# FFN up-projection by seven block products for eight in 21 of 22 tiles, with sums of X blocks made by token rows on VectorE

## The chip, the cores and the metric

The kernel runs on one core of one Trainium2 chip. The metric is the device time of one execution in microseconds, and the figure compared is the median of several runs. The core has five engines with a queue of instructions each: TensorE (PE in the profile), VectorE (DVE), ScalarE (ACT), GpSimd (POOL) and SyncE (SP, which here starts the DMAs). Each engine works its queue in order, and the engines wait for each other by semaphores.

## The reference

A trunk of two layers over 1024 tokens of 1024 channels, in float32. Each layer has a token mixer, a LayerNorm, and then the part that is changed:

```python
def conv_ffn(x, w_in, b_in, conv_w, conv_b, w_out, b_out):
    h = x @ w_in + b_in                       # 1024 x 5632
    hp = jnp.pad(h, ((0, 0), (1, 1), (0, 0)))
    h = hp[:, :-2] * conv_w[0] + hp[:, 1:-1] * conv_w[1] + hp[:, 2:] * conv_w[2] + conv_b
    u, g = jnp.split(h, 2, axis=-1)
    return (u * jax.nn.gelu(g, approximate=False)) @ w_out + b_out
...
        x = layer_norm(alpha * x + ff, ln_g[i, 1], ln_b[i, 1])
```

## The kernel before

A product of float32 matrices is made of three products of rounded parts: each operand is split into a high part (rounded to the type fp32r) and a low part (what the rounding left), and high by high, low by high and high by low are summed in PSUM. The input X of the FFN lies turned in SBUF as `XTh` and `XTl`: 128 channels of one of KT = 8 groups across the partitions, 1024 tokens along them.

`ffn_stage` runs once in each layer. The 2816 hidden channels of `u` and of `g` are FT = 22 tiles of 128. A tile f has a column block of `w_in` for u and one for g. `up_tile` (L1118) makes one of these two: for each half of the tokens, 8 channel groups times 3 products, so 48 matmuls of 128x512 into `ph`, and 96 for both. Then, for each tile:

- ScalarE (`take`, L1224) copies `ph` to `H` with the bias added, and to `C` with the middle tap of the convolution applied.
- VectorE (`conv`, L1284) adds the left tap (L1289) and the right tap (L1294), each one instruction of 128x1024 on `H` and `C` in SBUF.
- ScalarE applies GELU to the g half (`gate`, L1239), VectorE multiplies the halves (L1307), ScalarE rounds the product into `Ah` (`high`, L1243), VectorE makes the low part `Al` (`low`, L1311).
- After every second tile `down` (L1134) multiplies the two finished tiles by their rows of `w_out`: 16 outputs of 128x512, each 6 matmuls, in four PSUM banks `po` in turn. VectorE adds each output to the residual X (`add`, L1282). The output r waits until output r - 4 has been added. The last four tiles are summed in one go (`down_four`, L1157).

GpSimd prepares all weights: `split` (L1064) rounds 128x1024 weights of a DMA buffer `raw_weights` (two slots) into a high part (L1069, one input) and subtracts for the low part (L1071, two inputs). Three such splits belong to each tile. The order of everything is written out by hand. In the steady state a loop (`Fori`) holds a round of two up tiles, one `down` and their surroundings; its body is `round_` on TensorE (L1196). At the start of the stage GpSimd also adds the output bias to X (`add_bias`), between the splits, and ScalarE scales X by alpha (L1221).

## Time and profile before

| | us |
|---|---|
| median of 3 runs (2929.1 to 2930.05) | 2929.44 |
| the profiled execution, its own time | 2936.39 |
| its span in the trace | 2934.6 |
| PE busy (share of the span) | 2766.2 (94%) |
| DVE busy | 1644.1 (56%) |
| ACT busy | 993.6 (34%) |
| POOL busy | 1244.3 (42%) |
| mean granted TensorE clock | 0.972 |
| FFN of layer 0, first matmul to last part of the turned result | 799.5 to 1547.5 |
| FFN of layer 1, first matmul on | 2193.3 to the end |

A busy time is a sum of durations. A 128x512 matmul has a modelled duration of 390 ns, but one follows the other every 227 ns, so the cadence, not the duration, tells what a matmul costs. Idle time of an engine is put down to the engine or DMA that released it.

### The profile page before, as it was taken

The page shows a single profiled execution, that of the slowest core. Times are in us where ns is not written, and L with a number is a line of the kernel's source. Part 1 is how long each engine was busy: PE and PEld are TensorE (multiplying, and loading weights), DVE is VectorE, ACT ScalarE, POOL GpSimd, SP SyncE. Part 2 cuts the span into 40 slices and gives each one's busy share as a digit, 9 for nine tenths or more (in the row PEclk, how much of TensorE's full clock was granted, in tenths as well). Part 3 has the DMA queues.
Part 4 walks back from the last instruction along what each step waited for, and adds up shares of the span by engine and source line. Part 5 has one row for each costly group of instructions (what it writes and reads, how often), then busy time and mean ns, then how long its engine had stood idle before and what let it go on. Part 6 is the DMA issues. An engine that isn't in the chain of part 4 may idle for free. (4 is left out here: it accounts for less than half of the span.)

```text
span 2934.6 us, 36448 instructions
## 1 busy us (share of the span) xinstructions
PE 2766.2 (94%) x13387; PEld 2303.8 (79%) x13387; DVE 1644.1 (56%) x2106; ACT 993.6 (34%) x1402; POOL 1244.3 (42%) x890
## 2 busy tenths in 40 slices
PE   7999999977899999999998999998789999999998
PEld 6788888866788888888877888887668888888886
DVE  3676666663664444444473777777466444444446
ACT  3545554542231111221223555555323111222222
POOL 2444444323472333333354566654356233332335
PEclk9999999978999999999999999998899999999999
DMA  3100001225021111111121221211602111111111
GB/s 112 31 22 29 29 29 30 55 63 199 22 66 44 43 57 50 43 50 50 43 86 43 55 60 42 50 44 22 213 22 66 43 43 55 52 43 50 50 43 72
DMA packets 212649, 163.16 MB, mean 56 GB/s; under 512 B 34939, under 2 KB 194251, under 8 KB 212555
## 3 DMA queue, kind: packets, MB, share of 16 engines
q1 hardware_dynamic: 212411, 161.38, 18.6%
q8 instruction: 59, 0.97, 0.1%
q10 hardware_dynamic: 144, 0.52, 0.0%
q14 instruction: 35, 0.29, 0.0%
HBM read 137.24 MB, written 24.64 MB: 55 GB/s over the span
## 5 line engine op out<-in xcount | busy, mean ns | idle before, releaser
L1131 PE MATMUL ff_ph<-XTh,WH 128*128 128x512 f32 x1408 | 550.1, 391 | 6.8 <-PEq L41 6.8
L1131 PE MATMUL ff_ph<-XTl,WH 128*128 128x512 f32 x1408 | 549.3, 390 | 0.0
L1131 PE MATMUL ff_ph<-XTh,WL 128*128 128x512 f32 x1408 | 549.2, 390 | 0.0
L1289 DVE SCALAR_TENSOR_TENSOR ff_C<-ff_H,ff_par,ff_C 128x1024 f32<-128x1024 f32 x88 | 206.2, 2344 | 548.3 <-ACT ff_C L1233 548.3
L1069 POOL TENSOR_SCALAR WH<-raw_weights 128x1024 fp32r<-128x1024 f32 x128 | 142.2, 1111 | 847.1 <-PE ff_ph L1131 490.1
L1071 POOL TENSOR_TENSOR WL<-raw_weights,WH 128x1024 fp32r<-128x1024 f32 x128 | 328.7, 2568 | 10.7
L1131 PEld LDWEIGHTS ff_ph<-XTh,WH 128*128 128x128 f32 x1408 | 265.3, 188 | 62.7 <-issue 7.6
L1131 PEld LDWEIGHTS ff_ph<-XTh,WL 128*128 128x128 f32 x1408 | 265.2, 188 | 55.5
L1131 PEld LDWEIGHTS ff_ph<-XTl,WH 128*128 128x128 f32 x1408 | 265.4, 189 | 55.1
L1229 ACT ACTIVATE ff_H<-ff_ph,ff_par 128x1024 f32<-128x1024 f32 x88 | 98.4, 1118 | 553.7 <-PE ff_ph L1131 553.7
L1282 DVE TENSOR_TENSOR X<-ff_po,X 128x512 f32<-128x512 f32 x288 | 191.6, 684 | 102.5 <-PE ff_po L1145 102.5
L1145 PE MATMUL ff_po<-WH 128*128 128x512 f32 x576 | 228.2, 396 | 4.6
L1145 PE MATMUL ff_po<-WH,WL 128*128 128x512 f32 x576 | 224.5, 390 | 0.0
L1145 PE MATMUL ff_po<-WL,WH 128*128 128x512 f32 x576 | 224.3, 389 | 0.0
L547 ACT ACTIVATE da_E<-da_S,da_mn 128x1024 f32<-128x1024 f32 x128 | 142.9, 1117 | 227.8 <-DVE da_mn L660 225.0
L1526 POOL TENSOR_SCALAR na_E<-na_E,na_rden 128x512 f32<-128x512 f32 x128 | 104.7, 818 | 194.1 <-DVE na_rden L1869 193.4
L278 POOL TENSOR_SCALAR da_E<-da_E,da_rden,da_neglam 128x1024 f32<-128x1024 f32 x64 | 76.6, 1196 | 202.1 <-DVE da_rden L674 202.1
L347 PE MATMUL da_pa<-XTh,da_wh 128*128 128x512 f32 x360 | 152.2, 423 | 10.0 <-POOL da_wl L272 3.8
L660 DVE CUSTOM_DVE_ANT_0 da_S<-da_S,da_strip 128x1024 f32<-128x1024 f32 x128 | 153.8, 1241 | 8.1 <-PE da_S L361 8.0
L1612 PE MATMUL na_pa<-XTh,na_wh 128*128 128x512 f32 x360 | 145.6, 404 | 8.3 <-DVE na_wl L1847 6.9
L1243 ACT ACTIVATE WH<-ff_C 128x1024 fp32r<-128x1024 f32 x44 | 46.8, 1063 | 306.5 <-PE ff_po L1145 269.0
L347 PE MATMUL da_pa<-XTh,da_wl 128*128 128x512 f32 x360 | 144.1, 400 | 0.0
(224 smaller groups left out, 5993.4 us busy)
## 6 DMA issues: line engine op xcount, KB each, us to landing
raw_weights<-in_ffn_w_in SPq DMA_DIRECT2D x88, 512.0 KB, 3.8
raw_weights<-in_ffn_w_out SPq DMA_DIRECT2D x44, 512.0 KB, 3.6
raw_weights<-in_attn_w_qkv SPq DMA_DIRECT2D x24, 512.0 KB
raw_weights<-in_na_w_qkv SPq DMA_DIRECT2D x24, 512.0 KB, 4.4
wo_oraw<-heads_t SPq DMA_DIRECT2D x16, 512.0 KB, 4.4
rpb_rows<-da_rows SPq DMA_DIRECT2D x2, 3840.0 KB, 26.7
na_B<-rpb_rows SPq DMA_DIRECT2D x32, 224.0 KB, 4.3
da_E<-in_x SPq DMA_DIRECT2D x8, 512.0 KB, 5.7
```

The source lines that it names most:

```text
L347: last = nc.tensor.matmul(out[:], w[:, j // 2, k], x[:, k, t0:t0 + BANK], start=(i == 0), stop=(i == 3 * KT - 1))
L547: nc.scalar.activation(E[:, t % 2, c], Sc[c][:], ACT.Exp, scale=-1.0, bias=mn[:, t % 2, c:c + 1], accum_out=den[:, t % 2, c:c + 1]).then_i ...
L660: nc.vector.tensor_tensor_reduce(out=Sc[c][:], in0=Sc[c][:], in1=strip[:, (QT - 1 - t) * P:(QT - 1 - t) * P + S], scale=1.0, scalar=3.0e38 ...
L1069: nc.gpsimd.tensor_scalar(wh[:, slot], wraw[:, raw_slot], 1.0, 1.0, ALU.mult, ALU.mult).then_inc(w_high, 1)
L1071: nc.gpsimd.tensor_tensor(out=wl[:, slot], in0=wraw[:, raw_slot], in1=wh[:, slot].bitcast(F32), op=ALU.subtract).then_inc(w_low, 1)
L1131: last = nc.tensor.matmul(out[:, at], wt[:, slot, k * P:(k + 1) * P], x[:, k, at], start=(k == 0 and n == 0), stop=(k == KT - 1 and n == 2))
L1145: last = nc.tensor.matmul(po[r % 4][:], a[:, f, t * P:(t + 1) * P], wt[:, slots[f], half * BANK:(half + 1) * BANK], start=(f == 0 and n == ...
L1229: nc.scalar.activation(H[:, parity, 1:S + 1], ph[parity][:].rearrange("p k n -> p (k n)"), ACT.Identity, bias=par[:, 0, bass.ds(idx, 1)])
L1282: nc.vector.tensor_tensor(out=at, in0=po[r % 4][:], in1=at, op=ALU.add).then_inc(added, 1)
L1289: nc.vector.scalar_tensor_tensor(out=c, in0=h[:, 0:S], scalar=tap[1], in1=c, op0=ALU.mult, op1=ALU.add).then_inc(conv_link, 1)
L1526: nc.gpsimd.tensor_scalar(E[:, b], E[:, b], rden[:, b:b + 1], 1.0, ALU.mult, ALU.mult).then_inc(scaled, 1)
L1612: last = nc.tensor.matmul(out[:], w[:, j // 2, k], x[:, k, t0:t0 + BANK], start=(i == 0), stop=(i == 3 * KT - 1))
```

## The change

Tile 0 is made as before, with 96 matmuls, in four pieces (`up_plain`). For tiles 1 to 21 the product of a 256-column block (128 of u, 128 of g) by X is seen as a 2 by 2 by 2 block product (two gates, two halves of the channels, two halves of the tokens), and made by Strassen's scheme with seven products M1 to M7 of half-size blocks. `up_seven` has for each tile seven calls of `multiply`, each 4 channel groups times 3 products, 12 matmuls: 84 for 96.

What comes with it:

- Sums of weights (quads): five of the seven products need a sum or difference of two weight blocks, which GpSimd makes for every tile (`quad_add`). The rounding to the high part moves to ScalarE (`quad_copy`), the low part stays on GpSimd (`quad_lower`). They live in four slots (`SLOTS`). A quad takes its slot when the product four places earlier is made. All of these are 128x512. The rows of `w_out` are rounded on ScalarE (`down_copy`) and lowered on GpSimd (`down_lower`, 128x1024).
- Sums of X blocks, once in a stage: B1, B3, B4 and B7 are summed by token rows on VectorE (`mix_tokens`, 128x2048), turned by TensorE into PSUM (`turn_mix`, 16 transposes of 128x128 each), rounded by ScalarE (`mix_copy`) and lowered by VectorE (`mix_lower`). B6 is summed by TensorE (`sum_mix`, 16 matmuls of 128x512 with an identity).
- The results are put together from the products: ScalarE keeps M5 and M2 in SBUF (`keep`), VectorE forms U (`sum_u`, two instructions) and then `cross_take`, `main_prepare` and `main_take`, two of each, all 128x512 with one operand in PSUM. ScalarE reads the middle tap from `H` in SBUF (`centre_tap`) where it read PSUM.
- The loops are written out as straight code, and the LayerNorm's gain rows are loaded late in the stage.

```diff
+        token_mixes = {B1: (tokens(1, 1), tokens(2, 2), ALU.add, in_c), B3: (tokens(1, 2), tokens(2, 2), ALU.subtract, in_h),
+                       B4: (tokens(2, 1), tokens(1, 1), ALU.subtract, in_c), B7: (tokens(2, 1), tokens(2, 2), ALU.add, in_d)}
+        moving = {M5: quarter[2, 2], M2: quarter[1, 1], M1: places[B1], M3: places[B3], M4: places[B4],
+                  M7: quarter[2, 1], M6: quarter[1, 2]}
...
+            def quad_add(f, j):
+
+                n, i = f - PLAIN, index(f, j)
+                a, b, op = {M5: ((0, 1), (0, 2), ALU.add), M2: ((1, 1), (1, 2), ALU.add), M1: ((0, 1), (1, 2), ALU.add),
+                            M7: ((0, 2), (1, 2), ALU.subtract), M6: ((1, 1), (0, 1), ALU.subtract)}[j]
+                for gate, k in (a, b):
+                    pool.wait_ge(piece_in[2 * gate + k - 1], 16 * (n + 1))
+                if i >= SLOTS:
+                    pool.wait_ge(made, i - SLOTS + 1)
+                nc.gpsimd.tensor_tensor(out=Rf[:, i % SLOTS], in0=quad(*a), in1=quad(*b), op=op).then_inc(quad_sum, 1)
+
+            def quad_lower(f, j):
+
+                i = index(f, j)
+                pool.wait_ge(quad_high, i + 1)
+                src = quad(0, 1) if j == M3 else quad(1, 2) if j == M4 else Rf[:, i % SLOTS]
+                nc.gpsimd.tensor_tensor(out=Rl[:, i % SLOTS], in0=src, in1=Rh[:, i % SLOTS].bitcast(F32),
+                                        op=ALU.subtract).then_inc(quad_low, 1)
...
+            def next_quads(f):
+                quad_add(f, M5)
+                quad_add(f, M2)
+                quad_lower(f, M5)
+                quad_add(f, M1)
+                quad_lower(f, M2)
+                quad_lower(f, M1)
+                quad_lower(f, M3)
+
+            next_quads(PLAIN)
+            for t in range(TT):
+                add_bias(t)
+            for f in range(PLAIN, FT):
+                quad_lower(f, M4)
+                quad_add(f, M7)
+                quad_add(f, M6)
+                quad_lower(f, M7)
+                quad_lower(f, M6)
+                down_lower(f - 1)
+                if f + 1 < FT:
+                    next_quads(f + 1)
+            down_lower(FT - 1)
...
+            def multiply(f, j, out):
+
+                i = index(f, j)
+                pe.wait_ge(quad_low, i + 1)
+                xh, xl = moving[j]
+                for k in range(HK):
+                    wh, wl = (part[:, i % SLOTS, k * P:(k + 1) * P] for part in (Rh, Rl))
+                    for n, (w, x) in enumerate(((wh, xh), (wh, xl), (wl, xh))):
+                        last = nc.tensor.matmul(out, w, x[:, k], start=(k == 0 and n == 0),
+                                                stop=(k == HK - 1 and n == 2))
+                last.then_inc(made, 1)
...
+            def up_seven(f):
+
+                n = f - PLAIN
+                if n:
+                    pe.wait_ge(cross_h, 2 * n - 1)
+                else:
+                    pe.wait_ge(up_out, 2 * PLAIN)
+                multiply(f, M5, P12)
+                if n:
+                    pe.wait_ge(cross_h, 2 * n)
+                multiply(f, M2, P21)
+                if n:
+                    pe.wait_ge(main_h, 2 * n - 1)
+                else:
+                    sum_mix(B6)
+                    pe.wait_ge(mix_low, 2 * B1 + 2)
+                multiply(f, M1, P11)
+                pe.wait_ge(kept, 2 * n + 1)
+                if n == 0:
+                    pe.wait_ge(mix_low, 2 * B3 + 2)
+                multiply(f, M3, P12)
+                pe.wait_ge(kept, 2 * n + 2)
+                if n == 0:
+                    pe.wait_ge(mix_low, 2 * B4 + 2)
+                multiply(f, M4, P21)
+                pe.wait_ge(u_first, n + 1)
+                if n == 0:
+                    pe.wait_ge(mix_low, 2 * B7 + 2)
+                multiply(f, M7, P11)
+                if n:
+                    pe.wait_ge(main_h, 2 * n)
+                else:
+                    pe.wait_ge(mix_low, 2 * B6 + 2)
+                multiply(f, M6, P22)
...
+            up_plain(0, 0)
+            turn_mix(B1)
+            up_plain(0, 1)
+            turn_mix(B3)
+            up_plain(1, 0)
+            turn_mix(B4)
+            up_plain(1, 1)
+            turn_mix(B7)
+            for f in range(PLAIN, FT):
+                up_seven(f)
+                if f % 2 == 0 and f < FT - 2:
+                    down(f // 2 - 1)
+            down_four()
 
...
+            def centre_tap(f, parity):
+                n, idx = f - PLAIN, f + parity * FT
+                act.wait_ge(a_low, f)
+                act.wait_ge(cross_h, 2 * n + 1 + parity)
+                act.wait_ge(main_h, 2 * n + 1 + parity)
+                nc.scalar.activation(C[:, parity], H[:, parity, 1:S + 1], ACT.Identity, bias=par[:, 4, idx:idx + 1],
+                                     scale=par[:, 2, idx:idx + 1]).then_inc(tapped, 1)
...
+            for f in range(PLAIN, FT):
+                behind_down = f % 2 == 1 and 3 <= f < FT - 1
+                if behind_down:
+                    high(f - 1)
+                keep(f, M5)
+                quad_copy(f, M4)
+                keep(f, M2)
+                if f == PLAIN:
+                    mix_copy(B6)
+                quad_copy(f, M7)
+                quad_copy(f, M6)
+                if not behind_down:
+                    gate(f - 1)
+                if f < FT - 1:
+                    down_copy(f - 1)
+                if not behind_down:
+                    high(f - 1)
+                if f + 1 < FT:
+                    quad_copy(f + 1, M5)
+                    quad_copy(f + 1, M2)
+                    quad_copy(f + 1, M1)
+                else:
+                    down_copy(FT - 2)
+                    down_copy(FT - 1)
+                centre_tap(f, 0)
+                if f + 1 < FT:
+                    quad_copy(f + 1, M3)
+                centre_tap(f, 1)
+                if f % 2 == 0 and f < FT - 2:
+                    gate(f)
...
+                nc.vector.tensor_tensor(out=U, in0=P11, in1=part[:, 0], op=ALU.subtract).then_inc(u_first, 1)
...
+            def cross_take(f, parity):
+                idx = f + parity * FT
+                dve.wait_ge(made, index(f, M4 if parity else M3) + 1)
+                dve.wait_ge(conv_done, 2 * f - 1 + parity)
+                nc.vector.scalar_tensor_tensor(out=H[:, parity, here(1 - parity)], in0=(P12, P21)[parity],
+                                               scalar=par[:, 0, idx:idx + 1], in1=part[:, parity], op0=ALU.add,
+                                               op1=ALU.add).then_inc(cross_h, 1)
...
+            def main_take(f, parity):
+                n = f - PLAIN
+                dve.wait_ge(made, index(f, M6 if parity else M7) + 1)
+                dve.wait_ge(main_part, 2 * n + 2 - parity)
+                nc.vector.scalar_tensor_tensor(out=H[:, parity, here(parity)], in0=(P11, P22)[parity],
+                                               scalar=delta[:, parity, f:f + 1], in1=H[:, parity, here(parity)], op0=ALU.add,
+                                               op1=ALU.add).then_inc(main_h, 1)
```

On GpSimd, in the round of an even tile f. Before, three splits to a tile, each a rounding and a subtraction (two of them here, from the start of layer 1's stage, with the bias adds between); ff_bias is the output bias:

```order
L1069 TENSOR_SCALAR WH<-raw_weights 128x1024
L1071 TENSOR_TENSOR WL<-raw_weights,WH 128x1024
L1079 TENSOR_TENSOR X<-X,ff_bias 128x1024 x2
L1069 TENSOR_SCALAR WH<-raw_weights 128x1024
L1071 TENSOR_TENSOR WL<-raw_weights,WH 128x1024
```

Now, for one tile and the first quads of the next (ff_Rlf is the sum of weights, ff_Rh and ff_Rl its high and low part, ff_WDlf a row block of `w_out`):

```order
L1172 TENSOR_TENSOR ff_Rlf<-raw_weights 128x512 x2
L1179 TENSOR_TENSOR ff_Rl<-ff_Rlf,ff_Rh 128x512 x2
L1186 TENSOR_TENSOR ff_WDl<-ff_WDlf,ff_WDh 128x1024
L1172 TENSOR_TENSOR ff_Rlf<-raw_weights 128x512 x2
L1179 TENSOR_TENSOR ff_Rl<-ff_Rlf,ff_Rh 128x512
L1172 TENSOR_TENSOR ff_Rlf<-raw_weights 128x512
L1179 TENSOR_TENSOR ff_Rl<-ff_Rlf,ff_Rh 128x512 x2
L1179 TENSOR_TENSOR ff_Rl<-raw_weights,ff_Rh 128x512 x2
```

The roundings have left the engine, and twelve instructions of half the width with two inputs, and one of full width, stand for each tile.

On VectorE, around the same `down`. Before, the taps of an up tile stood close behind it and most of the adds to X behind them (ff_C is the convolved tile, ff_po the output of `down`):

```order
L1282 TENSOR_TENSOR X<-ff_po,X 128x512
L1294 ISA
L1294 SCALAR_TENSOR_TENSOR ff_C<-ff_H,ff_par,ff_C 128x1024
L1281 REGISTER_ALU
L1282 TENSOR_TENSOR X<-ff_po,X 128x512
L1281 REGISTER_ALU
L1282 TENSOR_TENSOR X<-ff_po,X 128x512
```

Now, from the last part of tile f - 1 on (ff_ph holds the seven products, ff_H the tile before its taps):

```order
L1542 TENSOR_TENSOR ff_C<-ff_C 128x1024
L1572 SCALAR_TENSOR_TENSOR ff_H<-ff_ph,ff_par,ff_part 128x512
L1580 TENSOR_TENSOR ff_H<-ff_po,ff_H 128x512
L1547 TENSOR_TENSOR WL<-ff_C,WH 128x1024
L1587 SCALAR_TENSOR_TENSOR ff_H<-ff_ph,ff_delta,ff_H 128x512 x2
L1531 SCALAR_TENSOR_TENSOR ff_C<-ff_H,ff_par,ff_C 128x1024
L1523 TENSOR_TENSOR X<-ff_po,X 128x512 x2
L1537 SCALAR_TENSOR_TENSOR ff_C<-ff_H,ff_par,ff_C 128x1024
L1523 TENSOR_TENSOR X<-ff_po,X 128x512 x2
```

The first add of a `down` (L1523) stands behind the left tap (L1531) of the tile that TensorE has only just finished, and that tap needs ScalarE's `centre_tap`.

On ScalarE, where `centre_tap` (L1443) stands in the even tile:

```order
L1426 ACTIVATE ff_Rh<-ff_Rlf 128x512 x2
L1392 ACTIVATE ff_C<-ff_C 128x1024
L1413 ACTIVATE ff_WDh<-ff_WDlf 128x1024
L1400 ACTIVATE WH<-ff_C 128x1024
L1426 ACTIVATE ff_Rh<-ff_Rlf 128x512 x3
L1443 ACTIVATE ff_C<-ff_H,ff_par 128x1024
L1426 ACTIVATE ff_Rh<-raw_weights 128x512
L1443 ACTIVATE ff_C<-ff_H,ff_par 128x1024
```

Three roundings of the next tile's sums (L1426) stand ahead of it, so it comes after GpSimd's third sum for the next tile.

## Rows read from the trace of the kernel before

**Rows 1.** Busy time in a stretch of the first FFN stage, each engine (instructions).
```profile
core 0: us, PE busy (x) PEld busy (x) DVE busy (x) ACT busy (x) POOL busy (x), PEclk, DMA share, GB/s
1000.00:1200.00 200.00, 199.20 (x872) 162.98 (x872) 88.96 (x84) 40.90 (x38) 66.35 (x38) 1.00 0.15 47
```

**Rows 2.** Chain of work that ended last: start, us, engine, tile, line, instructions.
```profile
2732.47 15.26 PE ff_po L1145 x66
2747.73 43.53 PE ff_ph L1131 x192
```

**Rows 3.** Waits in the first FFN stage: who for whom, us, times, longest.
```profile
PEld ff_po L1145 <- DVE X L1282: 10.0, 18, 0.6
```

**Rows 4.** Groups by form, VectorE, whole span.
```profile
L1289 DVE SCALAR_TENSOR_TENSOR ff_C<-ff_H,ff_par,ff_C 128x1024 f32<-128x1024 f32 x88 | 206.2, 2344 | 548.3 <-ACT ff_C L1233 548.3
L1282 DVE TENSOR_TENSOR X<-ff_po,X 128x512 f32<-128x512 f32 x288 | 191.6, 684 | 102.5 <-PE ff_po L1145 102.5
```

**Rows 5.** Single lines: durations ns min/median/max.
```profile
L1289 DVE SCALAR_TENSOR_TENSOR ff_C<-ff_H,ff_par,ff_C x88: 1285/2380/3407, 822.9 to 2881.4; 128x1024 f32<-128x1024 f32 x88
...
L1071 POOL TENSOR_TENSOR WL<-raw_weights,WH x128: 2387/2397/3337, 806.1 to 2880.5; 128x1024 fp32r<-128x1024 f32 x128
...
L1510 POOL TENSOR_TENSOR na_B<-na_colmask,na_B x16: 2112/2473/3092, 1559.7 to 2040.8; 128x896 f32<-128x896 f32 x16
```

**Rows 6.** In order of time, VectorE and GpSimd, 847 to 853 us.
```profile
847.86 1.47 DVE L1289 SCALAR_TENSOR_TENSOR ff_C<-ff_H,ff_par,ff_C 128x1024 f32<-128x1024 f32 x1 [0.51 <-ACT ff_C L1233]
848.34 3.24 POOL L1071 TENSOR_TENSOR WL<-raw_weights,WH 128x1024 fp32r<-128x1024 f32 x1
849.37 3.29 DVE L1294 SCALAR_TENSOR_TENSOR ff_C<-ff_H,ff_par,ff_C 128x1024 f32<-128x1024 f32 x1
```

**Rows 7.** Groups by form, ScalarE, whole span.
```profile
L1233 ACT ACTIVATE ff_C<-ff_ph,ff_centre,ff_par 128x1024 f32<-128x1024 f32 x88 | 105.6, 1200 | 7.7 <-DVE WL L1311 7.7
...
L1740 ACT ACTIVATE na_PT<-na_tb 128x512 fp32r<-128x512 f32 x128 | 76.4, 597 | 77.3 <-PE na_tb L1648 76.0
...
L1239 ACT ACTIVATE ff_C<-ff_C 128x1024 f32<-128x1024 f32 x44 | 46.7, 1060 | 190.2 <-DVE ff_C L1294 190.2
```

**Rows 8.** In order of time, TensorE, after waits of 2.6 and 3.8 us.
```profile
35.29 0.79 PE L347 MATMUL da_pa<-XTh,da_wh 128*128 128x512 f32 x1 [2.63 <-DVE XTl L583]
35.88 0.63 PE L347 MATMUL da_pa<-XTl,da_wh 128*128 128x512 f32 x1
36.31 0.63 PE L347 MATMUL da_pa<-XTh,da_wl 128*128 128x512 f32 x1
...
38.38 0.39 PE L347 MATMUL da_pa<-XTl,da_wh 128*128 128x512 f32 x1
38.61 0.39 PE L347 MATMUL da_pa<-XTh,da_wl 128*128 128x512 f32 x1
...
62.48 0.77 PE L347 MATMUL da_pa<-XTh,da_wh 128*128 128x512 f32 x1 [3.76 <-POOL da_wl L272]
...
65.60 0.39 PE L347 MATMUL da_pa<-XTl,da_wh 128*128 128x512 f32 x1
```

**Rows 9.** In order of time, TensorE, after two waits of 1.6 us.
```profile
158.14 1.09 PE L376 MATMUL da_tb<-ident,da_raw 128*128 128x128 f32 x8 [1.57 <-DVE da_ATl L608]
...
159.31 0.39 PE L347 MATMUL da_pa<-XTl,da_wh 128*128 128x512 f32 x1
...
310.03 1.09 PE L376 MATMUL da_tb<-ident,da_raw 128*128 128x128 f32 x8 [1.56 <-DVE da_ATl L608]
...
311.46 0.63 PE L347 MATMUL da_pa<-XTh,da_wl 128*128 128x512 f32 x1
```

**Rows 10.** In order of time, TensorE: transposes between matmuls.
```profile
23.52 1.91 PE L443 MATMUL da_S<-ident,da_E 128*128 128x128 f32 x16
```

**Rows 11.** DMA issues of the page: KB each, median us to landing.
```profile
raw_weights<-in_ffn_w_in SPq DMA_DIRECT2D x88, 512.0 KB, 3.8
```

More of the change, by code:

```diff
@@ new lines, in products @@
+            def products(out, r, f0, n, first, last_f):
+                t, half = r // 2, r % 2
+                for f in range(f0, f0 + n):
+                    (ah, al), (wh, wl, _) = a_slot(f), d_slot(f)
+                    for j, (a, w) in enumerate(((ah, wh), (ah, wl), (al, wh))):
+                        last = nc.tensor.matmul(out, a[:, t * P:(t + 1) * P], w[:, half * BANK:(half + 1) * BANK],
+                                                start=(f == first and j == 0), stop=(f == last_f and j == 2))
+                return last
@@ L1138, in down @@
+            def down(i):
+                pe.wait_ge(down_low, 2 * i + 2)
                 pe.wait_ge(a_low, 2 * i + 2)
                 for r in range(OUTS):
[L1140 to L1141 removed]
+                    if i or r >= 4:
                         pe.wait_ge(added, OUTS * i + r - 3)
[L1143 to L1147 removed]
@@ L1331, in add_last @@
+            f = FT - 1
+            left(f, 0), right(f, 0), left(f, 1), right(f, 1)
+            product(f)
+            low(f)
             def add_last(r):
```

584 lines of the change are left out of this document (353 added, 231 removed).

## The prediction

> **What bounds the kernel now.** I read the busy time by stretch first. In 200 us of an FFN stage TensorE is busy for 199.2 and starts 872 matmuls at a granted clock of 1.00, so one matmul costs 200 / 872 = 0.229 us there; VectorE is busy 44%, GpSimd 33%, ScalarE 20% [rows 1]. The chain of waits that ended last says the same: two tiles are 192 matmuls in 43.53 us, 0.227 each, and then a `down` [rows 2]. Over a round of 288 matmuls the two figures differ by 0.7 us. TensorE alone sets the time. Its only regular wait in the stage is for the adds of `down`, twice in each of the 9 `down`s of the stage [rows 3], and that is the 0.7. Matmuls taken away here are time won, as long as nothing else becomes late.
>
> So the second question is what else is near. The groups of VectorE have one odd figure: the left tap takes 2344 ns on average [rows 4], though the shortest of its kind took 1285 [rows 5]. The rows in order of time show why. At 848.34 GpSimd starts a subtraction, two inputs in SBUF; at 849.37 VectorE starts a right tap, also two inputs in SBUF. The tap ends at 852.66, 1.1 us after GpSimd's instruction (851.58), and GpSimd's own ran 3.24 where 2.39 is its shortest, since the tap before it ended only at 849.33 [rows 6]. Instructions of the two engines that both read two tensors in SBUF run one at a time, in order of arrival, each holding the other for about 1.07 us (a 1024 wide one of VectorE) or 2.25 us (GpSimd). VectorE's adds from PSUM are untouched: 684 ns on average [rows 4]. Nothing of this is on TensorE's path today.
>
> **The change part by part.** Sums are for one layer, then doubled.
>
> Matmuls removed: 21 tiles x 12 = 252, by 0.227 = -57.2 us. Added: `sum_mix` 16 x 0.227 = 3.6; four `turn_mix` of 16 transposes, 1.91 each [rows 10] = 7.6. Net on TensorE: -46.0 us.
>
> GpSimd: a tile has 12 instructions of 512 and one of 1024, all with two inputs. A 512 wide one is not in the trace. From 2112 ns at 896 and 2387 at 1024 [rows 5], 2.15 ns an element and 0.19 fixed, it is 1.29 us; the bounds are half of 2.39 (1.20) and 1.40, a fixed part of 0.4. A tile costs GpSimd 12 x 1.29 + 2.39 = 17.9 us, and TensorE needs 84 x 0.227 = 19.1 us for it. VectorE's six two-input instructions of a tile (four taps, product, low part) hold GpSimd off 6 x 1.07 = 6.4 us more: 24.3 us for a tile of 19.1 us. Over two tiles with a `down` (59.9 us) it fits, as does VectorE: 12 two-input ones of 1.3, 16 adds and 16 new 512 wide ones that read PSUM like the adds, 0.7 each, 38 us. In the even tile alone, which carries the odd tile's taps and comes before `down`, it does not.
>
> I walk that tile, T being the start of its M5. ScalarE's centre tap and quad copy after the previous M6, then GpSimd's lowering of M3 with one hold by a tap, bring GpSimd to the lowering of M4 at about T + 5.2. From there it has no free moment: nine instructions of 512 until the third sum for the next tile (lower M4, add M7, add M6, lower M7, lower M6, add M5, add M2, lower M5, add M1) = 11.6, the `w_out` one 2.4, and five holds by the right, left and right taps, product and low part, 1.07 less 0.12 that overlaps, = 4.7. The third sum ends at T + 23.9. ScalarE stands behind it: the copy 0.6 (512 wide, [rows 7]), then `centre_tap`, 1.06 plus 0.1 each for its bias and scale, 1.25 [rows 7]. VectorE's left tap follows, 1.3 and a 0.4 hold, then the first add 0.7. With 0.1 for handing over, less where instructions overlap, the add is done at T + 28. TensorE meets its wait for that add at output 4 of `down`: 19.1 + 24 x 0.227 = T + 24.5. Wait: 3.5 by 1.29, 3.2 by the mean with 1.25; I take 3.2.
>
> What such a wait costs beyond itself: after 2.63 us of waiting TensorE's matmuls followed each other every 0.43 us, from 35.29 to 38.38, and after 3.76 us from 62.48 to 65.60, where 0.23 is the rule [rows 8]: granted 1.2 GHz for 3.1 us, so 7 matmuls in the time of 14, 1.6 us lost. After 1.57 us the fall is the exception: 158.14 runs on at full level, 310.03 falls [rows 9]. At 3.2 I expect the fall each time. With 0.1 for the restart, a `down` costs 3.2 + 0.1 + 1.6 = 4.9, in 9 downs 44.1; the wait of today, 9 x 0.7, goes: +37.8 us.
>
> Two tile pairs have no `down` between them and both are heavy, 1 to 2 and 20 to 21. There M5 needs its low part, which GpSimd ends at about T + 22.4, where TensorE asks at T + 19.1: 3.0 + 1.6 each, the first partly in one slow stretch with others: +9 us.
>
> The start: after tile 0's last piece TensorE turns B7 (1.9) and waits for ScalarE, which has scaled four rows of X (four of 1.05) and then takes the second half (1.12 + 1.20 [rows 7]): about 2.8, a clock fall of 1.6 and 0.9 at an earlier turn: +5.3. The bias adds (8 on GpSimd) end before M4 of tile 1 needs its low part; they are covered by tile 0's 96 matmuls and cost nothing, and about 1 us a piece if that cover is short. The end: tile 21's taps, product, rounding and low part all come after its last product, against 48 matmuls (11 us) of cover: +1.
>
> DMAs: the quads are issued in halves of 256 KB. Today's 512 KB take 3.8 us to land [rows 11] and a slot is free at least 8 us ahead. The holds on SP's queue (a `w_out` load stands ahead of the next tile's pieces and waits for a `down` just finished) are covered; if they were not, each us would show as a wait at M5. The straight code for the loops: nothing, since the straight-line attention stage holds the same 0.23 cadence [rows 8].
>
> Sum: -46.0 + 37.8 + 9 + 5.3 + 1 = +7.1 us a layer, **+14.2** in all. The profiled execution took 2936.39 (1.8 beside its span), so 2950.6; it lies 7 above the median of the runs, 2929.44, and against that the same difference gives **2944**. This result is the difference of two large numbers, so its bounds matter: 0.05 us on the 512 wide instruction moves the wait by 0.5 us, and 18 waits by 9 us.
>
> A page of the Trainium skill bears on that instruction. The rows say 1.29 us, by a line through 896 and 1024 elements [rows 5]. GPSIMD Engine Reference, section "Elementwise — side-by-side cycle accounting", states 4497 ns for a two-input add of 2048 float32 against 2293 on VectorE, and advises VectorE for elementwise work. A line from that figure through the trace's 2387 at 1024 would make 512 wide 1.33 us, an estimate by that page, the waits 0.4 longer and the sum about +21. It speaks against the change, and the trace decides.
>
> **The rivals.**
>
> A. *The clock holds through the waits.* The waits are there, but TensorE comes back at 2.4 GHz as at 158.14 [rows 9]. Then 12 falls of 1.6 are missing in each layer: 7.1 - 19.2 = -12.1, twice -24: 2905. Against it: both waits of 2.6 us and more were followed by one [rows 8].
>
> B. *The waits are short.* If a 512 wide instruction takes 1.20 and handing over costs less, the chain is 1.5 us shorter: waits of about 1.7, clock mostly kept. -46.0 + 9 x 1.8 - 6.3 + 2 x 1.5 + 4 = -29 a layer: 2871, and up to 2905 if some fall. For it: nothing but the unmeasured 512. Against: 2112 at 896.
>
> C. *GpSimd and VectorE hold each other less at half width*, since a hold lasts half as long. Then only the start waits: -46.0 + 4 - 6.3 = -48 a layer: 2833. Against: a hold is per instruction, and GpSimd queues one behind the other.
>
> D. *GpSimd becomes the bound.* With 1.40 or more for a 512 wide one, or loads landing late, every tile pair waits at M5 too, and the `down` wait is 4.3: 9 x 1.1 + 9 x 0.8 = 17 more a layer: 2978. It decides from about 1.35 us.
>
> That the seven products are not what runs is excluded by the order of TensorE's queue.
>
> **How the numbers follow.** Forecast (2920 to 2962) 0.54; A 0.16; B 0.14; C 0.06; D 0.10. The predicted time is the forecast's, 2944. Its own range, 0.3 us on the wait either way (11) and 0.3 on what a fall costs (11), is 2920 to 2962 with both the same way. The range 2880 to 2975 leaves out C, half of D and part of B. A measurement tells 0.2%, 5.9 us, from no change. Slower: most of the forecast (0.47) and D, 0.57; same 0.07 from the forecast and 0.03 from A, 0.10; faster the rest, 0.33.
>
> **What would show it.** In the profile after: `multiply` matmuls 84 a tile at 0.227; GpSimd's 512 wide subtractions at 1.29 shortest and about 2.2 where held; a wait of TensorE for VectorE's add once in each `down`, about 3 us, 18 times, with `centre_tap` late behind the quad copies; the granted clock in the FFN stretches at 0.95 to 0.97 instead of 1.00. Wrong would be: no such wait, or a clock of 1.00 behind it (A), or waits at `multiply` in every tile (D).

## The result

The changed kernel took 2947.47 us (median of 4 runs, 2945.85 to 2950.84), the kernel before 2929.74 on the same chip (4 runs, 2929.10 to 2931.75). The ratio is 1.0061, 95% interval 1.0043 to 1.0078: slower by 0.6%. The profiled execution took 2948.5, its span 2946.7 at a mean granted clock of 0.962, where before had 0.972.

From a stage's first matmul to its last, the FFN stages took 745.4 and 729.4 us before (layer 0 and layer 1) and take 754.6 and 735.4 now: 9.2 and 6.0 us longer. The rest of the program took 3.1 us less in this execution than in that of before.

One stretch of the FFN stage, the same 200 us as [rows 1], and the stretch behind it, with the same columns:

```profile
1000.00:1200.00 200.00, 190.07 (x808) 155.16 (x807) 127.71 (x135) 65.72 (x86) 128.41 (x80) 0.97 0.17 50
1200.00:1400.00 200.00, 190.04 (x813) 155.15 (x812) 127.79 (x136) 64.71 (x85) 129.45 (x81) 0.97 0.16 48
```

TensorE stands idle for 9.9 us of 200 where it stood idle for 0.8, and its matmuls are slower too. 813 matmuls at the 0.2284 of [rows 1] (199.20 / 872) would be 185.7, and they took 190.04: 4.3 us lost in three rounds here, 5.5 (190.07 - 184.6) in the stretch before. VectorE went from 44% to 64%, GpSimd from 33% to 64%. What TensorE waits for in the FFN stages, whole span (who for whom, us in total, times, longest), answers to [rows 3]:

```profile
PE ff_po L1310 <- DVE X L1523: 57.9, 18, 3.3
...
PE ff_ph L1265 <- POOL ff_Rl L1179: 12.1, 4, 3.5
...
PE ff_ph L1265 <- ACT ff_C L1387: 5.2, 2, 2.6
...
PE ff_po L1310 <- DVE WL L1547: 3.7, 2, 2.2
```

The first line is the one of the 18 `down`s, at output 4, for VectorE's add. The second is M5 of tiles 2 and 21 of each layer, the third the start of tile 1, the fourth the end of the stage. Durations of GpSimd's lines (min/median/max in ns), for [rows 5]:

```profile
L1172 POOL TENSOR_TENSOR ff_Rlf<-raw_weights x210: 1261/1289/2299, 803.2 to 2879.4; 128x512 f32<-128x512 f32 x105
...
L1179 POOL TENSOR_TENSOR ff_Rl<-raw_weights,ff_Rh x84: 1280/2266/3344, 810.7 to 2874.9; 128x512 fp32r<-128x512 f32 x84
```

The chain behind one such wait, in order of time (start, us, engine, line). M5 of this even tile began at 1117.8, which is T of the prediction. The lower half of M4 is the second of the two instructions at 1120.88; the first took 2.29 us, so it starts at about 1123.1, T + 5.3. GpSimd, from there to its third sum:

```profile
1120.88 4.51 POOL L1179 TENSOR_TENSOR ff_Rl<-raw_weights,ff_Rh 128x512 fp32r<-128x512 f32 x2
1125.36 3.52 POOL L1172 TENSOR_TENSOR ff_Rlf<-raw_weights 128x512 f32<-128x512 f32 x2
1128.84 3.53 POOL L1179 TENSOR_TENSOR ff_Rl<-ff_Rlf,ff_Rh 128x512 fp32r<-128x512 f32 x2
1132.34 3.39 POOL L1186 TENSOR_TENSOR ff_WDl<-ff_WDlf,ff_WDh 128x1024 fp32r<-128x1024 f32 x1
1135.70 3.53 POOL L1172 TENSOR_TENSOR ff_Rlf<-raw_weights 128x512 f32<-128x512 f32 x2
1139.18 1.29 POOL L1179 TENSOR_TENSOR ff_Rl<-ff_Rlf,ff_Rh 128x512 fp32r<-128x512 f32 x1
1140.43 1.29 POOL L1172 TENSOR_TENSOR ff_Rlf<-raw_weights 128x512 f32<-128x512 f32 x1
```

No row has an idle time in brackets: GpSimd never stood still. Then ScalarE, VectorE and TensorE:

```profile
1141.76 0.63 ACT L1426 ACTIVATE ff_Rh<-ff_Rlf 128x512 fp32r<-128x512 f32 x1 [1.87 <-POOL ff_Rlf L1172]
1142.29 1.23 ACT L1443 ACTIVATE ff_C<-ff_H,ff_par 128x1024 f32<-128x1024 f32 x1
```
```profile
1143.55 1.73 DVE L1531 SCALAR_TENSOR_TENSOR ff_C<-ff_H,ff_par,ff_C 128x1024 f32<-128x1024 f32 x1 [5.42 <-ACT ff_C L1443]
1145.21 1.27 DVE L1523 TENSOR_TENSOR X<-ff_po,X 128x512 f32<-128x512 f32 x2
```
```profile
1145.94 0.50 PE L1310 MATMUL ff_po<-ff_WDh,WH 128*128 128x512 f32 x1 [3.32 <-DVE X L1523]
...
1147.72 0.63 PE L1310 MATMUL ff_po<-ff_WDh,WH 128*128 128x512 f32 x1
1148.14 0.63 PE L1310 MATMUL ff_po<-ff_WDl,WH 128*128 128x512 f32 x1
1148.57 0.63 PE L1310 MATMUL ff_po<-ff_WDh,WL 128*128 128x512 f32 x1
```

The copy of the third sum, the centre tap directly behind it, the left tap, the add, and TensorE after 3.32 us; then matmuls every 0.43 us, TensorE's lower level of 1.2 GHz, where 0.23 is the rule. VectorE stood idle for 5.42 us before the left tap: it is not the slow one, it is handed its input late.

### The profile page after: what moved, and what is told of

It is laid out like the page before. It is cut to its first block and busy times, and to the rows that moved or that the text cites. A ratio compares the mean times of both kernels' runs of the same rounds, so it can differ in the third digit from the quotient of the medians.

```text
span 2946.7 us, 35802 instructions
## 1 busy us (share of the span) xinstructions
PE 2703.4 (92%) x13043; PEld 2251.2 (76%) x13043; DVE 1919.8 (65%) x2474; ACT 1187.3 (40%) x1762; POOL 1654.8 (56%) x1182
## 5 line engine op out<-in xcount | busy, mean ns | idle before, releaser
L1179 POOL TENSOR_TENSOR ff_Rl<-raw_weights,ff_Rh 128x512 fp32r<-128x512 f32 x84 | 172.3, 2060 | 388.7 <-ACT ff_Rh L1426 388.7
L1172 POOL TENSOR_TENSOR ff_Rlf<-raw_weights 128x512 f32<-128x512 f32 x210 | 311.3, 1495 | 51.4 <-PE ff_ph L1265 36.9
L1310 PE MATMUL ff_po<-ff_WDh,WH 128*128 128x512 f32 x624 | 258.3, 414 | 57.9 <-DVE X L1523 57.9
L1426 ACT ACTIVATE ff_Rh<-ff_Rlf 128x512 fp32r<-128x512 f32 x210 | 132.8, 633 | 419.6 <-POOL ff_Rlf L1172 419.6
L1179 POOL TENSOR_TENSOR ff_Rl<-ff_Rlf,ff_Rh 128x512 fp32r<-128x512 f32 x210 | 291.3, 1404 | 0.0
L1265 PE MATMUL ff_ph<-XTh,ff_Rh 128*128 128x512 f32 x672 | 266.0, 396 | 17.4 <-POOL ff_Rl L1179 12.1
L1265 PE MATMUL ff_ph<-XTl,ff_Rh 128*128 128x512 f32 x672 | 264.5, 394 | 0.0
L1265 PE MATMUL ff_ph<-XTh,ff_Rl 128*128 128x512 f32 x672 | 264.0, 393 | 0.0
L1310 PE MATMUL ff_po<-ff_WDl,WH 128*128 128x512 f32 x624 | 253.4, 406 | 0.0
L1310 PE MATMUL ff_po<-ff_WDh,WL 128*128 128x512 f32 x624 | 252.9, 405 | 0.0
L1531 DVE SCALAR_TENSOR_TENSOR ff_C<-ff_H,ff_par,ff_C 128x1024 f32<-128x1024 f32 x88 | 155.9, 1772 | 144.5 <-ACT ff_C L1443 143.1
L1523 DVE TENSOR_TENSOR X<-ff_po,X 128x512 f32<-128x512 f32 x288 | 192.9, 685 | 80.5 <-PE ff_po L1310 80.1
L1265 PE MATMUL ff_ph<-WH,ff_Rl 128*128 128x512 f32 x504 | 196.1, 389 | 0.0
L1265 PE MATMUL ff_ph<-WL,ff_Rh 128*128 128x512 f32 x504 | 196.1, 389 | 0.0
```

The lines of the kernel that those rows point to most:

```text
L1172: nc.gpsimd.tensor_tensor(out=Rf[:, i % SLOTS], in0=quad(*a), in1=quad(*b), op=op).then_inc(quad_sum, 1)
L1179: nc.gpsimd.tensor_tensor(out=Rl[:, i % SLOTS], in0=src, in1=Rh[:, i % SLOTS].bitcast(F32), op=ALU.subtract).then_inc(quad_low, 1)
L1265: last = nc.tensor.matmul(out, w, x[:, k], start=(k == 0 and n == 0), stop=(k == HK - 1 and n == 2))
L1310: last = nc.tensor.matmul(out, a[:, t * P:(t + 1) * P], w[:, half * BANK:(half + 1) * BANK], start=(f == first and j == 0), stop=(f == las ...
L1426: nc.scalar.activation(Rh[:, i % SLOTS], src, ACT.Copy).then_inc(quad_high, 1)
L1523: nc.vector.tensor_tensor(out=at, in0=po[:, r % 4], in1=at, op=ALU.add).then_inc(added, 1)
```

## The experiments

The question is what makes the 18 waits, what each costs beyond itself, and where the gain of the smaller product count went. Theory 1 is the prediction's chain: GpSimd without a gap, held off by VectorE's two-input instructions; ScalarE's copies in order behind GpSimd's sums; the centre tap behind the copies; the left tap; the add; and a fall of the clock. The rivals are the place of the adds on VectorE, GpSimd's own throughput, and a clock that has nothing to do with these waits. Every kernel is a small edit of the changed kernel. The changed kernel itself was measured only on the first chip, at 1.0061 of the kernel before. So on a chip where before takes 2934.24 us the changed kernel is taken at 2952, and where before takes 2931.22 at 2949. By the interval of that ratio these two figures are good to about 5 us, and so are all differences from the changed kernel below. The slow intervals that are counted below are steps of about 0.43 us, in place of 0.23, from one matmul of a `down` to the next; each loses 0.2 us. In the changed kernel a fall of the clock follows 16 of the 18 waits, with 117 slow intervals in all.

### 1. The centre tap ahead of the quad copies (ScalarE)

```
+                early = f % 2 == 0 and f < FT - 2
+                if early:
+                    centre_tap(f, 0)
                 if f + 1 < FT:
                     quad_copy(f + 1, M5)
                     quad_copy(f + 1, M2)
                     quad_copy(f + 1, M1)
...
-                centre_tap(f, 0)
+                if not early:
+                    centre_tap(f, 0)
```

> One thing is changed against the changed kernel: in even tiles that have a `down`, ScalarE issues centre_tap(f, 0) before the three quad_copy of the next tile (M5, M2, M1) and not behind them. Theory 1 (the chain GpSimd's third sum, ScalarE's copy of it, centre tap, left tap, add sets the wait): the 18 waits of 3.3 us for VectorE's add at output 4 go, and the clock's fall behind each (5 to 13 intervals at 0.43 in place of 0.22 us, about 1.6 us) goes with them: 18 x 4.9 = 88 us less than the changed kernel's 2947.5, about 2859 us, unless the three copies, now later, make a new wait at M5 of the next tile. Rival (the place of the adds behind the left tap on VectorE is the cause, whatever ScalarE does): the wait stays above 2 us and the time above 2930 us. Rival (GpSimd as the bound, 105 us of work per pair of tiles): the time moves to M5 or M2 of the odd tiles, and the gain is under 20 us.

Measured: 2863.03 us (2862.39 to 2863.78) against 2934.24 of before, ratio 0.9760 (0.9745 to 0.9775). Against the changed kernel that is 89 us less, where 88 were expected. The line for VectorE's add is gone from TensorE's waits; those for GpSimd (12.1, 4 times) are as they were, so no new one took its place. In the middle of the layer TensorE is never idle:

```profile
1000.00:1200.00 200.00, 200.00 (x878) 164.02 (x877) 146.40 (x152) 68.00 (x90) 139.77 (x84) 1.00 0.16 48
1200.00:1400.00 200.00, 200.00 (x879) 164.32 (x879) 135.99 (x142) 70.08 (x93) 143.56 (x88) 1.00 0.19 58
```

The same place of an even tile, ScalarE and GpSimd in order of time:

```profile
1179.15 1.25 ACT L1443 ACTIVATE ff_C<-ff_H,ff_par 128x1024 f32<-128x1024 f32 x1 [3.03 <-DVE ff_H L1591]
1180.30 1.15 ACT L1426 ACTIVATE ff_Rh<-ff_Rlf 128x512 fp32r<-128x512 f32 x2
1184.30 0.63 ACT L1426 ACTIVATE ff_Rh<-ff_Rlf 128x512 fp32r<-128x512 f32 x1 [2.85 <-POOL ff_Rlf L1172]
```
```profile
1182.99 1.28 POOL L1172 TENSOR_TENSOR ff_Rlf<-raw_weights 128x512 f32<-128x512 f32 x1
```

The third sum starts at 1182.99, 3.8 us after the tap and 23.6 us after M5 of its tile, where it was 22.6 in the changed kernel. It is as late as ever, even 1.0 us later: the lower half before it waits 0.2 us for its copy and takes 2.0 us for 1.3, beside the left tap. It no longer matters: its product is due only after a whole `down` and two more products. The copies that moved behind the tap had room; the tap had none. GpSimd was not the bound; the order on ScalarE made its lateness count.

### 2. The adds ahead of the left tap (VectorE)

```
-                    left(f, 0)
                     ... add(done), add(done + 1)
+                    left(f, 0)
```

> One thing is changed against the changed kernel: VectorE issues the adds of outputs 0 and 1 of each `down` before the left tap of that tile and not behind it; centre_tap stays late. Theory 1: the left tap is still late by what centre_tap is late, and the adds of outputs 2 and 3 stand behind it, so the wait goes from output 4 to output 6, about 3 us long, less the left tap's own 0.7: 18 x 0.7 = 12 us less, about 2935 us. Rival (the adds' place is the cause): all 18 waits and their falls go, 2859 us.

Measured: 2944.41 us, ratio 1.0030 (1.0019 to 1.0040), 8 us less than the changed kernel where 12 were expected. TensorE's wait is still there 18 times, shorter by 0.5 us in the mean:

```profile
PE ff_po L1310 <- DVE X L1523: 49.2, 18, 2.9
```

The two adds that were freed only bring TensorE to the next two, which still stand behind the left tap: the wait is now at output 6. A fall follows all 18 waits, with 134 slow intervals for 117, so that about 3 us of the 8.7 that the waits lost went back to the clock. The place of the adds on VectorE is worth about 8 us of 89; the lateness of the tap is the rest.

### 3. Matmuls in the time of the wait

```
                 for r in range(OUTS):
                     ...
+                    if r == 4:
+                        for _ in range(14):
+                            nc.tensor.matmul(P12, plus[:], XTh[:, 0, 0:BANK], start=True, stop=True)
                     (wait for the add)
```

> Added to the changed kernel: 14 matmuls of 512 columns into a bank whose contents are not needed any more, in each `down` ahead of the wait at output 4 (about 14 x 0.22 = 3.1 us of the 3.3 us that TensorE stands idle). Nothing else moves, and the wait for the add ends when it did. If the clock falls because TensorE stands idle there, the 5 to 13 intervals at 0.43 us behind 17 of the 18 waits become 0.22 us: 17 x 1.5 = 26 us less, about 2921 us, and the span's mean granted clock goes from 0.96 to about 0.98. Rival (the falls are not from these waits, or the clock holds through such waits and the slow matmuls have another cause): about 2947 us or up to 5 us more, clock unchanged.

Measured: 2925.0 us (2922.05 to 2927.02), ratio 0.9969 (0.9958 to 0.9980), 27 us less with 252 matmuls more; 26 were expected. A stretch in the middle of the layer:

```profile
1200.00:1400.00 200.00, 199.49 (x873) 163.05 (x872) 129.16 (x138) 67.70 (x89) 132.03 (x83) 1.00 0.16 48
```

Granted clock 1.00 for 0.97, and 873 matmuls for 813, of which 14 a `down` are the added ones. No `down` has a slow interval. So of the 89 us of the waits, 27 are the clock's falls (the 117 slow intervals alone make 23) and about 62 the waits themselves (57.9, and what it takes to come back from them). Work that is thrown away made the kernel faster; the early tap shows that it is better not to wait.

### 4. Two of VectorE's instructions in the odd tile made short

This kernel leaves out nearly all of the right taps of the odd tiles, so its convolution isn't complete.

```
+                n = 16 if f % 2 == 1 and f < FT - 1 else S
-                ... scalar_tensor_tensor(out=C[:, parity], in0=H[:, parity, 2:S + 2], ...
+                ... scalar_tensor_tensor(out=C[:, parity, 0:n], in0=H[:, parity, 2:n + 2], ...
```

> Left out against the changed kernel: the right taps of the odd tiles' convolution, all but 16 of 1024 columns (two VectorE instructions for each pair of tiles), so part of the convolution isn't computed. This tells whether GpSimd's additions are late because VectorE's two-operand instructions hold them. Theory 1 (each such VectorE instruction of 1024 columns holds GpSimd's running instruction by about 1.0 us, and those of the odd tile push GpSimd's queue of the even tile back): the wait at output 4 shrinks from 3.3 to about 1.6 us, and half or more of the falls behind it go: 18 x 1.7 + 18 x 0.8 to 1.6 = 45 to 60 us less, 2885 to 2900 us. Rival (GpSimd's own work is the delay and VectorE's doesn't touch it): GpSimd's additions keep their mean durations, the wait stays at 3.3 us, and the time stays within 5 us of 2947.

Measured: 2886.54 us (2885.64 to 2887.86), ratio 0.9839 (0.9824 to 0.9854), 65 us less; 45 to 60 were expected. Nothing was taken from TensorE, from ScalarE or from GpSimd; only 40 VectorE instructions that ran beside them were cut to 16 of their 1024 columns, and the line of the wait is halved:

```profile
PE ff_po L1310 <- DVE X L1523: 28.0, 18, 1.6
```

GpSimd's subtractions from the raw quads, which run beside these taps, fell from a mean of 2060 to 1853 ns, those from the sums from 1404 to 1314. VectorE's work delays GpSimd's, and it comes out at TensorE. These waits account for 29.9 us, those for GpSimd at M5 (8.3 us for 12.1) for 3.8. The granted clock is 1.00 from 1000 to 1400 us, where the changed kernel has 0.97, and none of the 18 `down`s has a fall: behind waits of 1.6 us all of them went (27 by experiment 3), not half, which is the part that I had too low.

### 5. The tap one place later

```
                     quad_copy(f + 1, M5)
                     quad_copy(f + 1, M2)
+                    if f % 2 == 0 and f < FT - 2:
+                        centre_tap(f, 0)
                     quad_copy(f + 1, M1)
...
-                centre_tap(f, 0)
+                if f % 2 or f == FT - 2:
+                    centre_tap(f, 0)
```

> As the kernel of the early centre tap, but centre_tap(f, 0) stands one place later on ScalarE: behind quad_copy M5 and M2 of the next tile, ahead of M1 alone. Theory 1 (each copy holds the tap up until GpSimd's sum for it is there; the third sum alone accounts for over half of the 3.3 us): a `down` waits about 1.0 us at output 4 and 0.7 us at output 6, with few falls of the clock: 18 x 1.7 = 31 us more than the early tap, about 2894 us and about 55 us less than the changed kernel on the same chip. Rival (any place behind GpSimd's sums costs the same, since the sums stand ready together): the whole wait of 3.3 us is back and the time is near 2950 us. Rival (the third sum is the whole cause): no wait, 2863 us.

Measured: 2891.09 us (2889.18 to 2892.02), ratio 0.9860 (0.9844 to 0.9875), 58 us less than the changed kernel and 28 to 29 more than the early tap (ratios 0.9860 and 0.9760). The wait is now at two outputs and short:

```profile
PE ff_po L1310 <- DVE X L1526: 21.6, 34, 0.9
```

None of the 18 `down`s has a fall behind these waits, and the waits are shorter than the 1.7 us a `down` that were expected (21.6 / 18 = 1.2). With the tap behind no copy, two, or all three the kernel stands at 0.976, 0.986 and 1.006. The third sum alone is two thirds of the loss, which fits a chain with GpSimd's instructions as its links, and neither rival of this run.

### 6. and 7. One more addition on GpSimd, without and with the early tap

```
+                if j == M6 and f % 2 == 0:
+                    nc.gpsimd.tensor_tensor(out=Rf[:, i % SLOTS], in0=quad(*a), in1=quad(*b), op=op).then_inc(extra_done, 1)
+                    pool.wait_ge(extra_done, f // 2)
```

> Added to the changed kernel: one more GpSimd addition of two 128x512 operands (1.29 us alone) in each even tile, ahead of the sum for M6. Theory 1 (GpSimd's queue runs without a gap from the lower half of M4 to the third sum of the next tile, and a delay goes on to TensorE in full): 19 x 1.3 = 25 us more, 1.0 us of each as a new wait at M7 of the even tile and 0.4 us as a longer wait at output 4 (3.7 us): ratio to the kernel before about 1.015, near 2975 us. Rival (GpSimd has slack, being busy 56% of the span): no more than 3 us more, ratio 1.006.

> The kernel of the early centre tap with the same additional GpSimd addition in each even tile. If moving the tap took GpSimd off the critical path altogether, the time stays within 3 us of 2863. Theory 1: behind the tap there is no chain any more, but the lower half of M7 in the even tile still comes just in time, so that each pair of tiles waits 1.0 us there and a little behind it: 18 x 1.3 = 23 us more, about 2886 us, with a wait for GpSimd at M7 and none at output 4.

Measured with the early tap: 2885.22 us (2883.49 to 2886.43), ratio 0.9840 (0.9825 to 0.9855), 0.0080 or 23 us above the early tap alone. 23 were expected, and the new wait for GpSimd at a product is there, 18 times about 0.9 us on top of the four of before:

```profile
PE ff_ph L1269 <- POOL ff_Rl L1183: 28.8, 22, 3.6
```

So GpSimd does have a second place where it is just in time, M7 of the even tile, although it is busy for only 59% of the span.

Measured without the early tap: 2950.09 us (2945.45 to 2957.88), ratio 1.0058 (1.0042 to 1.0073), no more than the changed kernel's 1.0061. This missed: 1.015 was expected, and the number is the rival's 1.006. The rival's reason, that GpSimd has slack, is not what the trace shows, since the waits at M7 came as expected; those at output 4 did not grow by the expected 0.4 us (59.1 / 18 = 3.28 for 3.22):

```profile
PE ff_po L1314 <- DVE X L1527: 59.1, 18, 3.3
PE ff_ph L1269 <- POOL ff_Rl L1183: 28.9, 22, 3.6
```

These are 88.0 us for the 70.0 of the changed kernel. What gave most of that back is the clock: 7 of the 18 `down`s have a fall for 16, and 52 slow intervals for 117, about 13 us. In a stretch where both kernels wait 3.3 us in each `down`, the kernel with the addition, and behind it the changed one:

```profile
1120.00:1320.00 200.00, 187.42 (x818) 152.58 (x817) 124.67 (x134) 66.38 (x88) 133.58 (x87) 1.00 0.16 48
```
```profile
1120.00:1320.00 200.00, 190.04 (x813) 155.19 (x812) 128.42 (x135) 67.56 (x90) 129.43 (x81) 0.97 0.16 48
```

And one wait, with the matmuls behind it at 0.23 us from the first on:

```profile
1282.52 0.50 PE L1314 MATMUL ff_po<-ff_WDh,WH 128*128 128x512 f32 x1 [3.28 <-DVE X L1527]
1282.86 0.40 PE L1314 MATMUL ff_po<-ff_WDl,WH 128*128 128x512 f32 x1
1283.09 0.39 PE L1314 MATMUL ff_po<-ff_WDh,WL 128*128 128x512 f32 x1
1283.32 0.40 PE L1314 MATMUL ff_po<-ff_WDh,WH 128*128 128x512 f32 x1
```

The same wait for the same engine, and no fall. The falls that are left are in the first three `down`s of layer 0 and the first four of layer 1. The profiled execution was the longest of this kernel's four, 2957.88 us, and its span is 9.4 us longer than the changed kernel's, so how much of the 18 us came back is known only to some us. Two more kernels ask why the falls went.

### 8. and 9. Is it the length of the tile pair or the pause at M7 that keeps the clock up?

The first adds six matmuls behind the last output of each `down`, meant to make the pair of tiles as long as in experiment 6, with no pause at M7. The second is the kernel of experiment 6 with four matmuls in the pause at M7.

```
                     products(po[:, r % 4], r, 2 * i, 2, 2 * i, 2 * i + 1).then_inc(down_done, 1)
+                for _ in range(6):
+                    nc.tensor.matmul(P12, plus[:], XTh[:, 0, 0:BANK], start=True, stop=True)
```
```
+                if n and f % 2 == 0:
+                    for _ in range(4):
+                        nc.tensor.matmul(P11, plus[:], XTh[:, 0, 0:BANK], start=True, stop=True)
                 multiply(f, M7, P11)
```

> Added to the changed kernel: 6 matmuls of 512 columns into a bank that is not needed any more, behind the last output of each `down`, where TensorE doesn't wait: 18 x 6 x 0.227 = 24.5 us more work. In the kernel with the additional GpSimd addition TensorE stood 1.0 us longer in each pair of tiles, the waits at output 4 were still 3.3 us, and most falls of the clock behind them were gone, so that it took no longer. Theory A (a wait of 3.3 us brings a fall, whatever stands elsewhere in the pair of tiles): falls as in the changed kernel, granted clock 0.97 in the middle of the layer, ratio to the kernel before about 1.006 + 0.008 = 1.0145. Theory B (whether a fall comes hangs on where the waits stand in time, not on their length alone; the pair of tiles is now as long as in that kernel): waits of 3.3 us without falls, granted clock 1.00 in the middle of the layer, 24.5 - 18 x 1.4 = about 0 us more, ratio 1.005 to 1.008.

> The kernel with the additional GpSimd addition, and 4 matmuls of 512 columns (0.9 us) ahead of M7 in each even tile, into M7's own bank, in the time in which TensorE waited 1.0 us there. The pair of tiles keeps its length and the wait of 3.3 us at output 4; only the earlier pause is filled. If the distance of the waits in time decides whether the clock falls, nothing changes: granted clock 1.00 in the second half of the layer, ratio to the kernel before 1.006. If the earlier pause of 1.0 us was what kept the falls away, they are back, granted clock 0.97, and the time is 10 to 20 us longer: ratio 1.009 to 1.013.

Measured, six matmuls behind the outputs: 2973.47 us (2971.02 to 2975.78), ratio 1.0129 (1.0113 to 1.0146), 20 us above the changed kernel for 24.5 us of work. The 18 waits are as in the changed kernel (58.1 us in all), and so are the falls: 15 of 18 `down`s have one, with 113 slow intervals for 117. The interval of the ratio holds theory A's 1.0145 and not theory B's 1.005 to 1.008. A stretch in the middle of the layer:

```profile
1120.00:1320.00 200.00, 190.05 (x821) 155.36 (x820) 125.22 (x134) 64.11 (x84) 127.08 (x80) 0.98 0.16 50
```

Measured, the pause filled: 2954.96 us (2951.68 to 2957.72), ratio 1.0083 (1.0066 to 1.0099), its profiled span 2954.6 beside 2956.1 without the filling. The ratio lies between the two that were expected (1.006, and 1.009 to 1.013) and doesn't decide; the trace does. The falls did not come back, 5 of the 18 `down`s have one for 7 without the filling:

```profile
1120.00:1320.00 200.00, 190.17 (x829) 154.63 (x828) 125.52 (x135) 65.02 (x86) 133.52 (x86) 1.00 0.16 48
```

So the pause at M7 is not what keeps the clock up, and a wait's length alone is not either: four kernels have 18 waits of up to 3.3 us at the same place, and falls behind 16 (the changed kernel), 7 (experiment 6), 15 (experiment 8) and 5 (experiment 9) of them. Where the waits stand in time is left as a candidate, and it is not shown. From one wait to the next it is 64.8 us in the part of experiment 6 without falls and 64.9 in that of experiment 9, 65.2 with the falls in the changed kernel and 66.4 in experiment 8; but in experiment 8 a fall stood at 1353.72, 65.0 us after a wait without one, and in experiment 2 the waits follow each other every 64.8 us with a fall behind each. No one distance parts the two cases. The six matmuls were meant to set the distance alone and did not bring it about, so I can't say which distance does; this stays open.

### 10. The early tap and an earlier start

```
-                    pe.wait_ge(up_out, 2 * PLAIN)
+                    pe.wait_ge(up_out, 2 * PLAIN - 1)
                 multiply(f, M5, P12)
                 if n:
                     pe.wait_ge(cross_h, 2 * n)
+                else:
+                    pe.wait_ge(up_out, 2 * PLAIN)
```

> The kernel of the early centre tap, and at the head of each layer M5 of tile 1 waits for the first of ScalarE's two takes of tile 0 alone (its bank is the first that is free), and M2 for the second. The wait of 2.6 us for ScalarE at M5 goes; M1 then waits for its lower half about 1 us longer than it did at M5 of tile 2: about 2.3 us less a layer, 4 to 5 us less than the early tap alone, 2858 us. Rival (the wait only moves on to the next wait for GpSimd in tile 1 or 2): 2863 us.

Measured: 2859.09 us (2856.43 to 2859.98), ratio 0.9751 (0.9737 to 0.9764). The wait for ScalarE is gone, and GpSimd's went from 12.1 us in 4 to 14.4 in 5. The profiled spans differ by 3.9 us (2857.4 and 2861.3), as expected, but the intervals overlap, so that this step is not told from nothing with certainty. It is the fastest kernel of the study: 2.5% faster than the kernel before.

## Why the prediction was right

Forecast 2944, measured 2947.47; profiled execution forecast 2950.6, measured 2948.5. By its own steps:

- *The price of a 512 wide GpSimd instruction*, 1.29 us by the line through 896 and 1024, was the term on which everything hung. Measured: a median of 1289 ns for the sums and 1293 for the subtractions from them. The estimate of 1.33 by the figure in the Trainium skill's GPSIMD Engine Reference, section "Elementwise — side-by-side cycle accounting", was 3% too long. The totals don't tell its +21 from the +14 of the rows by themselves: the profiled executions differ by 12 (2948.5 less 2936.39), the FFN stages by 15.2, the medians by 17.7.
- *The walk through the even tile.* Lower half of M4 forecast at T + 5.2, third sum ended at T + 23.9, add done at T + 28, TensorE at output 4 at T + 24.5. With T = 1117.8: 5.3, 23.9 (1140.43 + 1.29), 28.1 (1145.94) and 24.8 (1145.94 - 3.32). The order of the chain is the one that was written down.
- *The wait*, 3.2: 57.9 / 18 = 3.22. It is 3.3 in eight of the first layer's nine and 2.5 in the first.
- *The fall behind it*, 1.6 each time: 1.4 to 1.8 for each round in the two stretches, 27 us in all by filling the wait, so 1.5 for each of 18. But the first `down` of a layer had none, one of the others had one twice as long (13 slow intervals), and experiment 6 shows that "each time" was luck of the arrangement. Both waits of [rows 8] had a fall and one of the two of [rows 9] had, and the spread between falling and not falling (27 us in the sum) is wider than the 11 us either way that I allowed for it. That 11 is also twice what its own terms give: 0.3 us on each of 18 waits is 5.4 in all, and as much for 18 falls, so that the two together make a range of 2933 to 2955; the measured time lies in that one too. Rival A, that the clock holds through such waits, had 0.16. It did not happen here, but in a kernel that differs by one addition it happens behind 11 of the 18 waits. Its weight was not too high.
- *The two tile pairs without a `down`*, 3.0 each: 12.1 / 4 = 3.0, 2.5 at tile 2 and 3.5 at tile 21. A fall stood behind three of the four, not behind layer 1's tile 21.
- *The start*, 2.8 for ScalarE: 2.6, with a fall of 5 or 6 slow intervals behind it, about 1.1 us for the 1.6. *The end*, +1: TensorE waited 1.85 us a layer for the last rounding there (3.7 / 2), a little more than given.
- *The net on TensorE*, -46.0 a layer. It can be read from the early tap: 2934.24 - 2863.03 = 71 us gained. By the prediction's terms, -46.0 + 9 + 5.3 + 1 - 6.3 = -37 a layer or -74. So the product count is worth what it was said to be, to about 3 us; the net itself was not measured apart from the other terms. A part of these 3 us can be the wait of today, put at 0.7 us a `down` or 6.3 a layer: with no wait there at all the early tap starts 878 matmuls in 200 us for 872 before, which is 1.4 us for three rounds, so nearer 0.5.
- *GpSimd and VectorE hold each other*: experiment 4 shows it by taking away only VectorE's part. In the stretch of the chain, from 1123.1 to 1141.7, nine instructions of 1.29 and one of 2.39 took 18.6 us, so 4.6 us were holds, where 4.7 were forecast. Rival C, that half width would free them, had little for it, and the median of 2266 ns beside the shortest of 1280 speaks against it: such an instruction is held for 1.0 us by a 1024 wide one of VectorE, nearly the forecast 1.07. But over the stage the holds are fewer than the six a tile that I counted: by the means less 1.29 and 2.39 they are 3.6 us a tile, not 6.4.
- *Rival D*, GpSimd as the bound, was nearer than its 0.10 says, and at another place than it named: 1.29 us more of GpSimd in an even tile makes TensorE wait at M7, 0.9 us each time, not at M5. Without it no product waits in the middle of a layer.

The other half of the prediction was an argument about the sum. Two large terms of opposite sign, -92 and +106, left +14, and the sign was right because the terms came out near their sizes: the 18 waits 57.9 us for 57.6, their falls 23 to 27 for 28.8, the M5 waits 12.1 for 12.0. The FFN stages grew by 9.2 and 6.0 us, where 7.1 a layer was forecast. With the falls gone, as in part of experiment 6, the sign would have been the other one, as the 2925.0 of experiment 3 shows; so the mechanism was right, and the sign had luck with the clock. A chance of 0.57 for slower was fair for that.

## What to carry to other kernels

When an engine's queue is in order, an instruction that is ready and urgent must not stand behind ones that wait for a busy engine: here one centre tap behind three copies cost 89 us, more than the 71 us that the change is worth without it. Read for each wait of the bound engine which instruction came last, then go up its engine's queue and ask of each that stands ahead of it when it is really needed. And when work is moved to engines that share operands' memory, count for each the instructions of the other that hold it, not its busy share.

## What was not expected of the hardware

Behind a wait of 3.3 us TensorE came back at 1.2 GHz for about 3 us in eight of nine `down`s of a layer, and in a kernel with one more addition on GpSimd it came back at 2.4 GHz after the same 3.3 us in 11 of 18: the granted clock from 1120 to 1320 us was 1.00 for 0.97, and 18 us of additional waiting left the time where it was to within some 5 us (ratio 1.0058 beside 1.0061). With the pause that the addition made filled, the clock was 1.00 still. Waits that were shorter, 2.8 us at output 6 in experiment 2 (2.0 in the first `down` of a layer), had a fall each time, 18 of 18, and those of 1.6 us in experiment 4 had none. A price of a fall that is read from single waits holds for those waits; for a sum over many, both cases belong in the range.
